# Joint gate-score levels and a four-quarter fp32 state readout in a hybrid RetNet/HGRN2 decoder step

## The chip, the cores and the metric

The kernel runs on one core of a Trainium2 chip. The metric is the device time of one execution in microseconds (us). TensorE (PE) does the matmuls; PEld are its weight loads; VectorE is DVE, ScalarE is ACT, GpSimd is POOL, and SyncE (SP) issues most of the transfers.

## The reference

One inference step of one decoder layer, in fp32, for 256 prompt tokens (one sequence) and 8 sample tokens (one new token of each of 8 running sequences). The model width is 2048.

```python
proj = rms_norm(x, norm_mix) @ w_in            # q,k,v,gate of retention; q,f,i,g of HGRN2; two merge gates
# retention, 8 heads, dk 128, dv 256, gamma_h = 1 - 2^(-5-h)
S = gamma * S + k^T v ;  o = q S               # per token; S starts at 0 (prompt) or at state_ret (samples)
# HGRN2, 8 heads, dk 128, dv 128
f = lb + (1 - lb) * sigmoid(z);  k = (1 - lb) * sigmoid(-z);  q = silu(hq)
S = diag(f) S + k^T i ;  o = S^T q
# both: RMS norm per head, swish gate, output projection; merged by two sigmoid gates, then w_out and residual
x = x + SwiGLU(rms_norm(x)) ;  y = rms_norm(x)
```

The new states (of the prompt and of each sample, for every head) are outputs too.

## The kernel before

The kernel keeps the activations transposed (features on 128 partitions, 264 tokens along the free axis: 256 prompt, then 8 sample tokens) and streams every weight matrix once, in chunks of 512 x 256 values (512 KB). SP loads a chunk into one of four ring slots (`raw`). ACT rounds it (`hi`, line 426), DVE forms the rest (`lo = raw - hi`, line 723), and PE multiplies hi*hi, hi*lo and lo*hi with 264 moving columns (lines 1082 to 1084): 24 matmuls for a chunk, in the reduced fp32r format, which streams a column per cycle. A slot is loaded again when DVE has split it, and `hi` is written again when PE has used the chunk.

The order of all work is written by hand. Each engine's program is a list of chunk numbers, with attention work hung behind certain chunks. The eight heads come first, 20 chunks ("steps" 0 to 19) each; head 0 stands apart and heads 1 to 7 are a loop. Then come the merge of both branches, the output projection and the feed-forward part. In a head:

- Step 3: DVE makes `forget`, `hkey`, `hquery` (lines 861 to 865) from PSUM, then hi/lo parts of the 8 sample keys and queries (`key_parts`, `query_parts`, lines 774 and 776), and spreads the query parts into a masked array with one used column per sample (`masked_query`, line 793). Step 7 does the same for retention. While step 3 runs, POOL norms the head before (lines 650 to 654) and then builds the gate products of this head.
- POOL (`levels`, lines 655 to 691): the causal decayed scores of HGRN2 are split into 7 levels. On level n, blocks of 2^n tokens look back at the block before. POOL forms `k_lev[n]` (keys of the first block of each pair times their decay; the other columns stay 0) and `q_lev[n]` for all 256 tokens, then the running products for the next level.
- SP loads the samples' old states `S_ret` (1 MB) and `S_hg` (512 KB) between the chunks of steps 13 and 14 (lines 371, 373).
- Steps 11 to 15 on PE: transposes of keys and values (line 1103), retention scores, the samples' rank-one updates (line 1113), outputs. Step 13's transposes wait for `v_parts` of DVE.
- Step 16 on PE: two diagonal score blocks (line 1187), then the level scores: 7 matmuls for the first 128 prompt tokens (line 1194) and 7 for the second 128 (line 1196). Each multiplies 128 columns of `k_lev` with all 128 columns of `q_lev`, of which 64 belong to its token block; DVE picks those with 7 predicated copies (line 934).
- Steps 14, 15, 17 on DVE: new sample states. ACT and DVE split them into `S_ret_hi/lo` and `S_hg_hi/lo` (lines 524, 532, 544, 809).
- Step 19 on PE, the readout (line 1224): for each of 8 samples and both parts of the state, one fp32r matmul of 16 stationary query columns (8 samples, hi and lo) with 256 (retention) or 128 (HGRN2) state columns, summed in PSUM rows 0 to 15. ACT copies these (`o16`, line 558). In the next head's step 0 (`tail`), PE turns them (lines 1124, 1126) and DVE adds the hi and lo rows (lines 817, 818).

```python
pe.wait_ge(state_split, h * 3 + 2)
for query, states, cols in ((q_only, (S_ret_hi, S_ret_lo), slice(0, RV)),
                            (hq_only, (S_hg_hi, S_hg_lo), slice(RV, 384))):
    for b in range(NS):
        for n, part in enumerate(states):
            last = mm(p7[0:2 * NS, 0, cols], query[:, b].rearrange("p c j -> p (c j)"), part[:, b, :], ...)
```

The large operands are placed at chosen address phases (`at_phase`), ahead of the heads' own arrays in memory.

Of the kernel before, what the change touches and what calls it, by code (L numbers as in the profile page):

```python
# [41 lines left out]
P = 128  # L42
# [45 lines left out]
K_IDENT = K_LEVEL + NLEV * 64  # L88
K_KDEC = K_IDENT + P
K_GAMMA = K_KDEC + 2 * H  # L90
K_EYE8 = K_GAMMA + H
K_ROW8 = K_EYE8 + NS * NS
# [14 lines left out]
def build(nc, consts, vectors, xT, w_in, w_ret, w_hg, w_out, w_fin, w_fout, s_ret, s_hg,  # L107
          yT, ret_p, hg_p, ret_s, hg_s):
    with ExitStack() as ctx:
# [35 lines left out]
        lb_tmp = alloc(heads, "lb_tmp", [P, 4, H])  # L145
        norm_tmp = ExitStack()
# [5 lines left out]
        hkey = alloc(heads, "hkey", [P, T])  # L152
        hquery = alloc(heads, "hquery", [P, T])
# [17 lines left out]
        q_parts = alloc(heads, "q_parts", [P, NS, 2], F32R)  # L171
        hq_parts = alloc(heads, "hq_parts", [P, NS, 2], F32R)

        q_only = alloc(heads, "q_only", [P, NS, 2, NS], F32R)
        hq_only = alloc(heads, "hq_only", [P, NS, 2, NS], F32R)
        o16 = alloc(heads, "o16", [2 * NS, 384])
# [8 lines left out]
        k_lev = [alloc(heads, f"k_lev{i}", [P, NP]) for i in range(NLEV)]  # L185
# [17 lines left out]
        S_ret_hi = alloc(heads, "S_ret_hi", [P, NS, RV], F32R)  # L203
        S_ret_lo = alloc(heads, "S_ret_lo", [P, NS, RV], F32R)
        S_hg_hi = alloc(heads, "S_hg_hi", [P, NS, HV], F32R)
        S_hg_lo = alloc(heads, "S_hg_lo", [P, NS, HV], F32R)
# [32 lines left out]
        c_level = cst[:, K_LEVEL:K_LEVEL + NLEV * 64].bitcast(I32).rearrange("p (l j) -> p l j", l=NLEV)  # L239
        c_kdec = cst[:, K_KDEC:K_KDEC + 2 * H].rearrange("p (b h) -> p b h", b=2)  # L240
        c_eye8 = cst[:, K_EYE8:K_EYE8 + NS * NS].rearrange("p (b j) -> p b j", b=NS)
# [41 lines left out]
        hg_sig_done = sem("hg_sig_done")  # L283
        products = sem("products")
# [6 lines left out]
        state_hi = sem("state_hi")  # L291
        state_split = sem("state_split")
# [120 lines left out]
        def _(act):  # L413
# [58 lines left out]
            def head(h, first=False):  # L472
# [3 lines left out]
                for i in range(HEAD_CHUNKS):  # L476
# [38 lines left out]
                    elif i == 15:  # L515

                        act.wait_ge(b_free, h * 2 + 3)
                        fn(hg_sig[:], hig[:, 1, :], ACT.Sigmoid).then_inc(hg_sig_done, 1)
# [4 lines left out]
                        act.wait_ge(p56_free, h * N56 + (OUT1 + 2))  # L523
                        copy(S_ret_hi[:, 0:4, :], S_ret[:, 0:4, :]).then_inc(state_hi, 1)
                    elif i == 16:
# [4 lines left out]

                        act.wait_ge(p56_free, h * N56 + (OUT1 + 3))
                        copy(S_ret_hi[:, 4:8, :], S_ret[:, 4:8, :]).then_inc(state_hi, 1)
                    elif i == 18:
# [8 lines left out]

                        act.wait_ge(p56_free, h * N56 + (OUTH4 + 2))
                        copy(S_hg_hi[:], S_hg[:]).then_inc(state_hi, 1)
                    elif i == 19:

                        act.wait_ge(a_free, h * 3 + 4)
                        fn(rg_sig[:], rg_gate[:], ACT.Sigmoid).then_inc(rg_sig_done, 1)


                        act.wait_ge(state_split, h * 3 + 3)
# [5 lines left out]
                        act.wait_ge(p7_full, h * N7 + (RD3 + 1))  # L557
                        copy(o16[:], p7[0:2 * NS, 0, 0:384]).then_inc(p7_free, 1)
# [65 lines left out]
        def _(pool):  # L624
            tt = nc.gpsimd.tensor_tensor
            pool.sem_inc(normed, 4)

# [15 lines left out]
            for i in range(NLEV):  # L643
                nc.gpsimd.memset(k_lev[i][:], 0.0).then_inc(products, 1)

            steps = 2 + 4 * NLEV + 4
# [10 lines left out]
            def levels(h):  # L657

                count = [NLEV]
# [13 lines left out]
                for i in range(NLEV):  # L673
# [6 lines left out]
                    shape = [P, NP // (2 * s), s]  # L680
# [3 lines left out]
                    step(tt(kl0, k0, g0, ALU.mult))  # L684
# [6 lines left out]
                step(tt(kbar, hkey[:, 0:NP], run_g[:], ALU.mult))  # L691
                assert count[0] == NLEV + steps
# [22 lines left out]
        def _(dve):  # L715
# [56 lines left out]
            def parts(hi_out, lo_out, x, h, n):  # L772

                nc.vector.tensor_copy(hi_out, x).then_inc(parts_done, 1)
                dve.wait_ge(parts_done, h * 14 + (2 * n + 1))
# [11 lines left out]
            def query_parts(out, x, h, n):  # L787
                parts(out[:, :, 0], out[:, :, 1], x, h, n)
# [14 lines left out]
            def level_psum(n):  # L803

                return bass.AP(tensor=p56, offset=64 * n, ap=[[2 * 512, P], [512 + 64, 2], [1, 64]])

            def state_lo(out, state, state_hi_part, h, n):
                dve.wait_ge(state_hi, h * 3 + (n + 1))
                tt(out, state, state_hi_part.bitcast(F32), ALU.subtract).then_inc(state_split, 1)

            def tail(i, h):

                if i == 0:

                    dve.wait_ge(p4_full, h * N4 + (TO4 + 1 - N4))
                    by_part = p4[:, 0, 0:48].rearrange("p (e two b) -> p e b two", e=3, two=2)
                    nc.vector.tensor_reduce(oT[:, :, NP:T], by_part[:, 0:2], AX.X, ALU.add).then_inc(sample_outputs, 1)
                    nc.vector.tensor_reduce(ohT[:, NP:T], by_part[:, 2], AX.X, ALU.add).then_inc(sample_outputs, 1)
# [8 lines left out]
            def head(h, first=False):  # L827
# [3 lines left out]
                for i in range(HEAD_CHUNKS):  # L831
# [26 lines left out]
                    if i == 3:  # L858
# [4 lines left out]
                        ts(hkey[:], z_nsig[:], omlb[:, bass.ds(h, 1)], None, ALU.mult).then_inc(forget_done, 1)  # L863
                        dve.wait_ge(a_free, h * 3 + 2)
# [3 lines left out]
                        query_parts(hq_parts, hquery[:, NP:T], h, 1)  # L868
                        dve.wait_ge(parts_done, h * 14 + 4)
                        masked_query(hq_only[:], hq_parts[:])  # L870
                    elif i == 7:
# [8 lines left out]
                        key_parts(k_parts, qk[:, 1, NP:T], h, 2)  # L880
                        query_parts(q_parts, qk[:, 0, NP:T], h, 3)
                        dve.wait_ge(parts_done, h * 14 + 8)
                        masked_query(q_only[:], q_parts[:])
                    elif i == 11:

                        dve.wait_ge(a_free, h * 3 + 3)
                        for e in range(2):
                            value_parts(v_parts[:, e], vT[:, e, NP:T], h, 4 + e)
                        dve.wait_ge(keys_copied, h + 1)
                        masked_keys(k_only[:], p7[0:8 * NS, 0, 256:384])  # L890
                        dve.wait_ge(masked, h * 3 + 3)
# [7 lines left out]
                    elif i in (14, 15):  # L899
# [9 lines left out]
                        if i == 15:  # L909

                            dve.wait_ge(b_free, h * 2 + 3)
                            value_parts(v_parts[:, 2], hig[:, 0, NP:T], h, 6)
                            state_lo(S_ret_lo[:, 0:4, :], S_ret[:, 0:4, :], S_ret_hi[:, 0:4, :], h, 0)
                    elif i == 16:
# [3 lines left out]
                           c_ident.rearrange("p (a n) -> p a n", a=1).broadcast_to([P, 2, P]), ALU.mult  # L918
                           ).then_inc(score_step, 1)
# [5 lines left out]
                        for n in range(NLEV):  # L925
# [4 lines left out]
                            msk = c_level[:, n:n + 1, :].rearrange("p a (b s) -> p a b s", s=s  # L930
                                                                   ).broadcast_to([P, 2, 64 // s, s])
# [4 lines left out]
                    elif i == 17:  # L936
# [7 lines left out]
                        state_lo(S_ret_lo[:, 4:8, :], S_ret[:, 4:8, :], S_ret_hi[:, 4:8, :], h, 1)  # L944
                    elif i == 18:
                        state_lo(S_hg_lo[:], S_hg[:], S_hg_hi[:], h, 2)

# [123 lines left out]
        def _(pe):  # L1071
# [26 lines left out]
            steps = 2 + 4 * NLEV + 4  # L1098

            def natural(out, src, width):  # L1100

                for b in range(2):
                    last = transpose(out[:, b * width:b * width + 128], src[:, b * P:b * P + P], c_ident)
# [5 lines left out]
            def sample_updates(q, h):  # L1109

                pe.wait_ge(masked, h * 3 + 3)
# [5 lines left out]
            def tail(i, h):  # L1117

                if i == 0:
# [3 lines left out]
                    one16 = c_ident[0:2 * NS, 0:2 * NS]  # L1123
# [12 lines left out]
            def attend(i, h):  # L1136

                if i == 11:

                    pe.wait_ge(p7_free, h * N7 + (TK0 + 1))  # L1140
                    pe.wait_ge(parts_done, h * 14 + 6)
# [7 lines left out]
                elif i == 13:  # L1149

                    pe.wait_ge(p56_free, h * N56 + (TV0 + 1))
                    pe.wait_ge(parts_done, h * 14 + 12)
# [24 lines left out]
                elif i == 16:  # L1177

                    pe.wait_ge(products, h * steps + (NLEV + steps))
                    pe.wait_ge(p7_free, h * N7 + (TI2 + 1))  # L1180
                    pe.wait_ge(parts_done, h * 14 + 14)
                    natural(p7[:, 0, 0:256], hig[:, 0, :], 128)
# [3 lines left out]
                    for b in range(2):  # L1186
                        mm(p4[:, 0, b * P:b * P + P], hkey[:, b * P:b * P + P], hquery[:, b * P:b * P + P],
                           start=True, stop=True)
# [194 lines left out]
```

## Time and profile before

| what | value |
|---|---|
| median of 3 runs (lowest to highest) | 1834.14 us (1831.59 to 1836.6) |
| the profiled execution's own time | 1834.16 us |
| its span, first to last instruction | 1832.3 us |
| mean granted TensorE clock | 0.995 |
| PE busy / PEld busy | 1785.3 us (97%) / 1766.0 us (96%) |
| DVE / ACT / POOL busy | 1147.5 (63%) / 776.9 (42%) / 277.4 us (15%) |
| HBM traffic over the span | 182 GB/s |

Matmuls are pipelined, and the duration of one record reaches past the start of the next. What a group of matmuls costs PE is therefore read from start to start. A matmul of plain fp32 operands shows as two records (each with its weight load), one of fp32r operands or a transpose as one. The name of an array in a row is without its number (`k_lev` for `k_lev0` to `k_lev6`; `p` for PSUM).

### The profile page before, as it was taken

How to read it: one execution, taken by the hardware profiler on the slowest of the kernel's cores; microseconds unless marked ns; L12 is line 12 of the kernel's file. 1: busy time of each engine (PE TensorE's matmuls, PEld its weight loads, DVE VectorE, ACT ScalarE, POOL GpSimd, SP SyncE). 2: the span in 40 equal slices, each digit the busy share in tenths (PEclk: the TensorE clock that was granted, in tenths of full speed). 3: DMA queues.
4: the chain of work that ended last, by engine and by line, in shares of the span. 5: the costliest groups of instructions: out<-in, count | busy, mean ns of one | idle time of the engine just before them, and what ended most of it. 6: DMA issues, size and time to landing. Idle time of an engine off the chain costs nothing.

```text
span 1832.3 us, 37809 instructions
## 1 busy us (share of the span) xinstructions
PE 1785.3 (97%) x14672; PEld 1766.0 (96%) x14672; DVE 1147.5 (63%) x1293; ACT 776.9 (42%) x894; POOL 277.4 (15%) x332
## 2 busy tenths in 40 slices
PE   5999999999999999999999999999999999999997
PEld 5999999999999999999999999999999999999996
DVE  8776877778777675555556665555555555545444
ACT  5454544445444454344444444444444444333332
POOL 4442614416144110000000000000000000000001
PEclk9999999999999999999999999999999999999998
DMA  7665646666466555555547665555565565555552
GB/s 230 192 202 177 197 139 197 190 183 196 140 193 191 184 163 185 184 183 183 182 153 245 192 183 183 182 180 181 181 182 182 183 182 182 185 184 177 179 182 102
DMA packets 388538, 333.86 MB, mean 182 GB/s; under 512 B 11776, under 2 KB 386560, under 8 KB 388352
## 3 DMA queue, kind: packets, MB, share of 16 engines
q1 hardware_dynamic: 369536, 318.88, 56.3%
q10 hardware_dynamic: 18944, 14.16, 2.5%
q8 instruction: 43, 0.70, 0.2%
q14 instruction: 15, 0.12, 0.0%
HBM read 316.67 MB, written 16.32 MB: 182 GB/s over the span
## 4 chain that ended last, share of the span: by engine, by line
PE 82%; DVE 7%; issue 4%; DMA 3%; SPq 2%; ACT 1%; DVEq 0%; POOL 0%; ACTq 0%
PE pA L1082 13%; PE pA L1084 12%; PE pA L1083 12%; PE pB L1082 10%; PE pB L1084 10%; PE pB L1083 10%; PE p L1082 3%; PE p L1084 3%; PE p L1083 3%; DMA raw<-in_w_in 2%; DVE lo L723 2%; PE p L1224 1%; SPq L348 1%; DVE hg_scores L934 1%; SPq L373 1%
## 5 line engine op out<-in xcount | busy, mean ns | idle before, releaser
L723 DVE TENSOR_TENSOR lo<-raw,hi 128x1024 fp32r<-128x1024 f32 x568 | 723.6, 1279 | 557.2 <-ACT hi L426 549.0
L426 ACT CAST hi<-raw 128x1024 fp32r<-128x1024 f32 x568 | 595.2, 1048 | 826.9 <-PE pA L1084 347.2
L1082 PE MATMUL pA<-h_hi,hi 128*128 128x264 f32 x1728 | 499.8, 289 | 19.0 <-DVE lo L723 18.7
L1083 PE MATMUL pA<-h_lo,hi 128*128 128x264 f32 x1728 | 492.0, 285 | 0.0
L1084 PE MATMUL pA<-h_hi,lo 128*128 128x264 f32 x1728 | 491.9, 285 | 0.0
L1082 PE MATMUL pB<-h_hi,hi 128*128 128x264 f32 x1472 | 421.6, 286 | 0.0
L1083 PE MATMUL pB<-h_lo,hi 128*128 128x264 f32 x1472 | 417.2, 283 | 0.0
L1084 PE MATMUL pB<-h_hi,lo 128*128 128x264 f32 x1472 | 417.2, 283 | 0.0
L1082 PEld LDWEIGHTS pA<-h_hi,hi 128*128 128x128 f32 x1728 | 327.7, 190 | 22.6 <-issue 18.9
L1083 PEld LDWEIGHTS pA<-h_lo,hi 128*128 128x128 f32 x1728 | 327.8, 190 | 0.3
L1084 PEld LDWEIGHTS pA<-h_hi,lo 128*128 128x128 f32 x1728 | 327.6, 190 | 0.0
L1082 PEld LDWEIGHTS pB<-h_hi,hi 128*128 128x128 f32 x1472 | 277.3, 188 | 0.3
L1083 PEld LDWEIGHTS pB<-h_lo,hi 128*128 128x128 f32 x1472 | 277.4, 188 | 0.2
L1084 PEld LDWEIGHTS pB<-h_hi,lo 128*128 128x128 f32 x1472 | 277.2, 188 | 0.0
L703 POOL TENSOR_TENSOR x<-x,vec 128x528 f32<-128x528 f32 x8 | 12.2, 1524 | 1151.2 <-DVE sq L1058 1151.2
L1082 PE MATMUL pA<-hid_hi,hi 128*128 128x264 f32 x352 | 99.9, 284 | 2.3 <-issue 2.3
L1082 PE MATMUL pB<-hid_hi,hi 128*128 128x264 f32 x352 | 100.3, 285 | 0.0
L1083 PE MATMUL pB<-hid_lo,hi 128*128 128x264 f32 x352 | 100.1, 284 | 0.0
L1084 PE MATMUL pB<-hid_hi,lo 128*128 128x264 f32 x352 | 100.1, 284 | 0.0
L1083 PE MATMUL pA<-hid_lo,hi 128*128 128x264 f32 x352 | 99.7, 283 | 0.0
L1084 PE MATMUL pA<-hid_hi,lo 128*128 128x264 f32 x352 | 99.5, 283 | 0.0
L1082 PE MATMUL p<-ro_hi,hi 128*128 128x264 f32 x256 | 72.7, 284 | 1.2 <-DVE ro_lo L979 1.2
(250 smaller groups left out, 2483.6 us busy)
## 6 DMA issues: line engine op xcount, KB each, us to landing
raw<-in_w_fin SPq DMA_DIRECT2D x176, 512.0 KB, 3.7
raw<-in_w_in SPq DMA_DIRECT2D x128, 512.0 KB, 3.5
raw<-in_w_in SPq DMA_DIRECT2D x192, 256.0 KB, 3.9
raw<-in_w_fout SPq DMA_DIRECT2D x88, 512.0 KB, 3.5
raw<-in_w_ret SPq DMA_DIRECT2D x32, 512.0 KB, 4.3
raw<-in_w_out SPq DMA_DIRECT2D x32, 512.0 KB, 4.2
S_ret<-in_s_ret SPq DMA_DIRECT2D x8, 1024.0 KB, 8.4
out_ret_s<-S_ret ACTq DMA_DIRECT2D x8, 1024.0 KB, 7.0
```

The lines of the kernel that those rows point to most:

```text
L348: sp.dma_start(raw[s][:, :, 0:128], half(i, first, col, 0)).then_inc(raw_full[s], 16)
L373: sp.dma_start(S_hg[:], s_hg[:, bass.ds(h, 1), :, :].rearrange("b h d e -> d (b h) e")).then_inc(state_in_hg, 16)
L426: copy(hi[s], raw[s]).then_inc(hi_done, 1)
L703: tt(x2[:, 2 * g:2 * g + 2, :], x2[:, 2 * g:2 * g + 2, :], vec[:, V_FINAL + 2 * g:V_FINAL + 2 * g + 2].rearrange("p (k a) -> p k a", a=1). ...
L723: tt(lo[s], raw[s], hi[s].bitcast(F32), ALU.subtract).then_inc(split_done, 1)
L934: last = nc.vector.copy_predicated(dst, msk, src)
L1082: mm(outs[t][:, ::-1], w_hi, a_hi[:, kt, ::-1], start=(kt == 0), stop=False)
L1083: mm(outs[t][:, ::-1], w_hi, a_lo[:, kt, ::-1], start=False, stop=False)
L1084: last = mm(outs[t][:, ::-1], w_lo, a_hi[:, kt, ::-1], start=False, stop=(kt == CK * n - 1))
L1224: last = mm(p7[0:2 * NS, 0, cols], query[:, b].rearrange("p c j -> p (c j)"), part[:, b, :], start=(b == 0 and n == 0), stop=(b == NS - 1 ...
```

## The change

Level scores. Both token blocks go into one matmul per level. The keys of the second 128 tokens are written in reverse order (`[:, ::-1]`), so that they fall on the columns that the first block's keys leave unused; `k_lev[n]` shrinks to 128 columns, nothing in it has to be zero, and its products are two half-size POOL instructions in place of one. The reversed keys and values of the second block come from two new arrays: `hkey_back` (DVE, step 3) and `hval_back` (ACT, step 15, which PE's step 16 waits for). The masks, no longer the same for both blocks, get twice as wide in the constants, and the second diagonal block uses a reversed identity.

Readout. The states stay in plain fp32, so their four splits and the two query splits go. The 8 samples are put into four groups of 32 stationary columns. Group g writes PSUM rows 32g to 32g+31 through `tile_position=(0, 32 * g)`, first for sample g, then, summed, for sample 4+g. The query arrays are cleared once at the start and DVE then writes only the 8 used columns of each. ACT copies 128 rows, PE turns them with three full transposes, and DVE copies the used columns instead of adding pairs. ACT issues the two state stores after that copy and no longer before it.

```diff
-            def masked_query(out, q):
-                shape = [P, NS, 2, NS]
-                tt(out, q.bitcast(F32).rearrange("p b (c a) -> p b c a", a=1).broadcast_to(shape),
-                   c_eye8.rearrange("p b (a j) -> p b a j", a=1).broadcast_to(shape), ALU.mult).then_inc(masked, 1)
+            def place_queries(out, q):
+                return nc.vector.tensor_copy(
+                    out[:, :, 0:128].rearrange("p r (g j) -> p r g j", g=4)[:, :, :, 0],
+                    q.rearrange("p (r g) -> p r g", r=2)).then_inc(queries_placed, 1)
...
                         ts(hkey[:], z_nsig[:], omlb[:, bass.ds(h, 1)], None, ALU.mult).then_inc(forget_done, 1)
+                        ts(hkey_back[:], z_nsig[:, P:NP][:, ::-1], omlb[:, bass.ds(h, 1)], None, ALU.mult)
                         dve.wait_ge(a_free, h * 3 + 2)
                         tt(hquery[:], hqf[:, 0, :], hq_sig[:], ALU.mult).then_inc(forget_done, 1)
                         dve.wait_ge(forget_done, h * 3 + 3)
                         key_parts(hk_parts, hkey[:, NP:T], h, 0)
-                        query_parts(hq_parts, hquery[:, NP:T], h, 1)
-                        dve.wait_ge(parts_done, h * 14 + 4)
-                        masked_query(hq_only[:], hq_parts[:])
+                        place_queries(hq_only, hquery[:, NP:T])
...
-                    step(tt(kl0, k0, g0, ALU.mult))
+                    tt(kl0, k0[:, 0:n], g0[:, 0:n], ALU.mult).then_inc(products, 1)
+                    step(tt(kl1, k0[:, n:], g0[:, n:], ALU.mult))
...
                     for n in range(NLEV):
-                        mm(p56[:, 0, 64 * n:64 * n + P], k_lev[n][:, 0:P], q_lev[n][:], start=True, stop=True)
-                    for n in reversed(range(NLEV)):
-                        last = mm(p56[:, 1, 64 * n:64 * n + P], k_lev[n][:, P:NP], q_lev[n][:], start=True, stop=True)
+                        last = mm(p56[:, n // 4, (n % 4) * P:(n % 4) * P + P], k_lev[n][:], q_lev[n][:],
+                                  start=True, stop=True)
...
-                        copy(S_hg_hi[:], S_hg[:]).then_inc(state_hi, 1)
-                        state_lo(S_hg_lo[:], S_hg[:], S_hg_hi[:], h, 2)
...
-                    pe.wait_ge(state_split, h * 3 + 2)
+                    pe.wait_ge(queries_placed, h * 2 + 2)
+                    pe.wait_ge(p56_free, h * N56 + (OUTH4 + 2))
+                    for query, state, cols in ((q_only, S_ret, slice(0, RV)), (hq_only, S_hg, slice(RV, 384))):
+                        rows = query[:].rearrange("p r x -> p (r x)")
+                        for r in range(2):
+                            for g in range(4):
+                                b = 4 * r + g
+                                last = mm(p7[32 * g:32 * g + 32, 0, cols], rows[:, 32 * b:32 * b + 32], state[:, b, :],
+                                          start=(r == 0), stop=(r == 1), tile_position=(0, 32 * g))
...
-                    mm(p4[:, 0, 0:16], o16[:, 0:128], one16, start=True, stop=True)
-                    for e in range(1, 3):
-                        last = transpose(p4[:, 0, 16 * e:16 * e + 16], o16[:, e * 128:e * 128 + 128], one16)
+                    for e in range(3):
+                        last = transpose(p4[:, 0, e * P:e * P + P], o_rows[:, e * P:e * P + P], c_ident)
```

## Rows read from the trace of the kernel before

Heads are numbered 0 to 7. The stretches of rows 3 run from ACT's first square root in one head's step 2 to the same place in the next.

**Rows 1.** the page's part 1: busy time of each engine

```profile
PE 1785.3 (97%) x14672; PEld 1766.0 (96%) x14672; DVE 1147.5 (63%) x1293; ACT 776.9 (42%) x894; POOL 277.4 (15%) x332
```

**Rows 2.** the list of waits, engine PE: line, releaser, us in total, times, longest

```profile
PE p L1103 <- DVE v_parts L776: 8.2, 6, 1.6
...
PE p L1203 <- DVE hg_scores L934: 1.9, 8, 0.3
```

**Rows 3.** stretches of head 1 and head 7: us, busy by engine

```profile
107.40:182.50 75.10, 74.72 (x610) 72.69 (x609) 56.22 (x78) 35.57 (x49) 31.29 (x38) 1.00 0.63 185
...
565.60:642.40 76.80, 74.96 (x610) 72.71 (x609) 56.85 (x78) 35.53 (x49) 29.79 (x38) 1.00 0.59 180
```

**Rows 4.** chain that ended last, head 7 from step 14: start us, us, what

```profile
609.35 0.43 PE p L1170 x2
...
615.62 1.56 PE p L1194 x14
...
630.09 2.84 PE p L1224 x32
```

**Rows 5.** timeline of PE at step 14: start us, us, instruction

```profile
604.45 0.28 PE L1084 MATMUL pB<-h_hi,lo 128*128 128x264 f32 x1
604.66 0.74 PE L1113 MATMUL p<-v_rows,k_only 32*128 32x256 f32 x4
605.33 1.13 PE L1164 MATMUL p<-v_nat,kd_nat 128*128 128x256 f32 x4
```

**Rows 6.** timeline of PE, step 19: readouts of 256, then 128 columns

```profile
553.11 0.28 PE L1224 MATMUL p<-S_ret_hi,q_only 128*16 128x256 f32 x1
...
554.99 0.22 PE L1224 MATMUL p<-S_hg_hi,hq_only 128*16 128x128 f32 x1
```

**Rows 7.** weight loads of the readout: ns min/median/max, first and last start

```profile
L1224 PEld LDWEIGHTS p<-S_ret_hi,q_only x64: 93/95/96, 94.8 to 631.5; 128*16 128x16 f32 x64
```

**Rows 8.** timeline of PE: transposes of step 11, then of the tail

```profile
592.36 0.28 PE L1084 MATMUL pA<-h_hi,lo 128*128 128x264 f32 x1
...
592.48 0.38 PE L1103 MATMUL p<-cst,qk 128*128 128x128 f32 x2
...
592.93 0.28 PE L1083 MATMUL pB<-h_lo,hi 128*128 128x264 f32 x1
...
635.59 0.28 PE L1084 MATMUL pA<-h_hi,lo 128*128 128x264 f32 x1
...
636.47 0.28 PE L1083 MATMUL pA<-h_lo,hi 128*128 128x264 f32 x1
```

**Rows 9.** chain that ended last, head 7, between steps 3 and 14

```profile
589.27 6.07 DMA raw<-in_w_in
```

**Rows 10.** timeline of DVE in step 3, head 1, then head 7

```profile
117.49 0.42 DVE L865 TENSOR_TENSOR hquery<-hqf,hq_sig 128x264 f32<-128x264 f32 x1
...
120.70 5.49 DVE L723 TENSOR_TENSOR lo<-raw,hi 128x1024 fp32r<-128x1024 f32 x4
...
575.37 0.35 DVE L863 TENSOR_SCALAR hkey<-z_nsig,omlb 128x264 f32<-128x264 f32 x1
...
575.64 1.55 DVE L865 TENSOR_TENSOR hquery<-hqf,hq_sig 128x264 f32<-128x264 f32 x1
...
578.24 0.67 DVE L774 CAST hq_parts<-hquery 128x8 fp32r<-128x8 f32 x1
...
579.57 5.48 DVE L723 TENSOR_TENSOR lo<-raw,hi 128x1024 fp32r<-128x1024 f32 x4
```

**Rows 11.** groups by line and shape: DVE's split of the new states

```profile
L809 DVE TENSOR_TENSOR S_ret_lo<-S_ret,S_ret_hi 128x1024 fp32r<-128x1024 f32 x16 | 19.5, 1221 | 0.0
```

**Rows 12.** timelines, head 7: POOL, last product; PE, step 16

```profile
602.58 1.60 POOL L691 TENSOR_TENSOR rg_sig<-hkey,run_g 128x256 f32<-128x256 f32 x1
...
614.24 0.38 PE L1103 MATMUL p<-cst,hig 128*128 128x128 f32 x2
```

**Rows 13.** DMA issues: queue, count, KB each, median us to landing

```profile
cst<-in_consts SPq DMA_DIRECT2D x1, 1888.0 KB, 9.0
```

More of the change, by code:

```diff
@@ L145, in build @@
         lb_tmp = alloc(heads, "lb_tmp", [P, 4, H])
+        q_only = alloc(heads, "q_only", [P, 2, NS * 16 + 1])
+        hq_only = alloc(heads, "hq_only", [P, 2, NS * 16 + 1])
         norm_tmp = ExitStack()
@@ L152, in build @@
         hkey = alloc(heads, "hkey", [P, T])
+        hkey_back = alloc(heads, "hkey_back", [P, P])
+        hval_back = alloc(heads, "hval_back", [P, P])
         hquery = alloc(heads, "hquery", [P, T])
@@ L184, in build @@
         S_hg = alloc(heads, "S_hg", [P, NS, HV])
-        k_lev = [alloc(heads, f"k_lev{i}", [P, NP]) for i in range(NLEV)]
+        k_lev = [alloc(heads, f"k_lev{i}", [P, P]) for i in range(NLEV)]
         run_f = alloc(heads, "run_f", [P, NP])
@@ L517, in head @@
                         act.wait_ge(b_free, h * 2 + 3)
+                        copy(hval_back[:], hig[:, 0, P:NP][:, ::-1]).then_inc(hval_turned, 1)
                         fn(hg_sig[:], hig[:, 1, :], ACT.Sigmoid).then_inc(hg_sig_done, 1)
@@ L642, in _ @@
             pool.wait_ge(h_done, 4)
-            for i in range(NLEV):
-                nc.gpsimd.memset(k_lev[i][:], 0.0).then_inc(products, 1)
-            steps = 2 + 4 * NLEV + 4
+            steps = 2 + 5 * NLEV + 5
             def last_outputs(h):
@@ L679, in levels @@
                     kl0, _ = halves(k_lev[i][:], s)
-                    shape = [P, NP // (2 * s), s]
+                    kl1, _ = halves(k_lev[i][:, ::-1], s)
+                    n, shape = P // (2 * s), [P, NP // (2 * s), s]
                     if i:
@@ L690, in levels @@
                 step(tt(run_g[:, 0:P], run_g[:, 0:P], run_f[:, NP - 1:NP].broadcast_to([P, P]), ALU.mult))
-                step(tt(kbar, hkey[:, 0:NP], run_g[:], ALU.mult))
-                assert count[0] == NLEV + steps
+                tt(kbar[:, 0:P], hkey[:, 0:P], run_g[:, 0:P], ALU.mult).then_inc(products, 1)
+                count[0] += 1
+                step(tt(kbar[:, P:NP][:, ::-1], hkey[:, P:NP], run_g[:, P:NP], ALU.mult))
+                assert count[0] == steps
             levels(0)
@@ L803, in level_psum @@
             def level_psum(n):
[L805 to L809, printed above, removed]
+                return p56[:, n // 4, (n % 4) * P:(n % 4) * P + P].rearrange("p (k j) -> p k j", k=2)
             def tail(i, h):
@@ L1096, in _, with natural @@
                 pe.sem_inc(free, 1)
-            steps = 2 + 4 * NLEV + 4
-            def natural(out, src, width):
+            steps = 2 + 5 * NLEV + 5
+            def natural(out, src, width, second=None):
                 for b in range(2):
-                    last = transpose(out[:, b * width:b * width + 128], src[:, b * P:b * P + P], c_ident)
+                    block = src[:, b * P:b * P + P] if second is None or b == 0 else second
+                    last = transpose(out[:, b * width:b * width + 128], block, c_ident)
                 return last
@@ L1177, in attend @@
                 elif i == 16:
-                    pe.wait_ge(products, h * steps + (NLEV + steps))
+                    pe.wait_ge(products, h * steps + steps)
                     pe.wait_ge(p7_free, h * N7 + (TI2 + 1))
-                    pe.wait_ge(parts_done, h * 14 + 14)
-                    natural(p7[:, 0, 0:256], hig[:, 0, :], 128)
+                    pe.wait_ge(parts_done, h * 10 + 10)
+                    pe.wait_ge(hval_turned, h + 1)
+                    natural(p7[:, 0, 0:256], hig[:, 0, :], 128, second=hval_back[:])
                     natural(p7[:, 0, 256:512], kbar, 128).then_inc(p7_full, 1)
@@ L1186, in attend @@
                     for b in range(2):
-                        mm(p4[:, 0, b * P:b * P + P], hkey[:, b * P:b * P + P], hquery[:, b * P:b * P + P],
-                           start=True, stop=True)
+                        mm(p4[:, 0, b * P:b * P + P], hkey_back[:] if b else hkey[:, 0:P],
+                           hquery[:, b * P:b * P + P], start=True, stop=True)
                     mm(p4[:, 0, 256:384], k_top, q_lev[NLEV][:], start=True, stop=True)
@@ L1215, in attend @@
                 elif i == 19:
-                    pe.wait_ge(state_split, h * 3 + 2)
-                    for query, states, cols in ((q_only, (S_ret_hi, S_ret_lo), slice(0, RV)),
-                                                (hq_only, (S_hg_hi, S_hg_lo), slice(RV, 384))):
-                        if query is hq_only:
-                            pe.wait_ge(state_split, h * 3 + 3)
-                        for b in range(NS):
-                            for n, part in enumerate(states):
-                                last = mm(p7[0:2 * NS, 0, cols], query[:, b].rearrange("p c j -> p (c j)"),
-                                          part[:, b, :], start=(b == 0 and n == 0), stop=(b == NS - 1 and n == 1))
+                    pe.wait_ge(queries_placed, h * 2 + 2)
[7 more added lines that the diff above has]
+                                          start=(r == 0), stop=(r == 1), tile_position=(0, 32 * g))
                     last.then_inc(p7_full, 1)
```

90 lines of the change are left out of this document (37 added, 53 removed).

## The prediction

> **What bounds the kernel now.** I read the page first. PE is busy for 1785.3 of 1832.3 us [rows 1], so what counts is which matmuls go, and where PE still waits. The list of PE's waits has, past the start, one large entry: step 13's transposes wait 8.2 us for DVE's `v_parts`, and 1.9 us are waited for the predicated copies [rows 2]. The windows by head place the first: head 1 takes 75.1 us, head 7 76.8 with the same PE work, and heads 2 to 6 are like head 7 (76.4 to 76.8) [rows 3]. Everything else that the change takes from DVE and ACT lies beside a busy PE. All edits lie in the eight heads, the first 640 us or so; after them nothing changes.
>
> **Level scores.** PE runs 14 records (7 fp32 matmuls) at line 1194 in 1.56 us, and as many at line 1196 [rows 4]. One set goes; the other keeps its shape, 128 by 128. 8 x 1.56 = **-12.5 us**. PE is next busy with chunk 17, so nothing takes the gap. DVE's copies start at the end of the last level matmul as before, and the 1.9 us behind them stay. POOL gets eight more instructions in a head (seven levels and `kbar`, each product in two halves). Its last product ends at 604.2 and PE first needs them at 614.24 [rows 12]: 10 us of cover, enough even at 1.2 us for each addition; beyond that PE would wait at step 16 one for one. `hval_back` is a small ACT copy early in step 15, covered by chunk 16 (24 matmuls at 0.12 us = 2.9 us) and by the ACT cast of the state that leaves the same step. Both at nothing. The wider masks make the constants 256 KB larger; at 1888 KB in 9.0 us [rows 13] that is 1.2 us in front of chunk 4's load, three chunks ahead of PE's need of it: between 0 and +1.2, I take 0.
>
> **Readout.** Before: 32 fp32r matmuls in 2.84 us [rows 4], 0.1175 us apart where they stream 256 columns ((554.99 - 553.11) / 16 [rows 6]). After: 16 plain fp32 matmuls, that is 32 records. Plain fp32 costs 0.43 / 2 = 0.215 us per record at 256 columns (line 1170) and 1.56 / 14 = 0.111 at 128 [rows 4]. One behind the other: 16 x 0.215 + 16 x 0.111 = 5.22 us. All four quarters side by side: a quarter, 1.31 us. No row shows two column groups at work at once, so these are the two ends. Between them: records start in program order in every timeline, and the two records of one matmul use the same 32 columns. The second then waits out the first, and the next group's first record, queued behind it, can only run beside that second one. So matmuls pair up: 8 x 0.215 + 8 x 0.111, and a last record of 0.111, = 2.72 us. A change to a narrower tile also costs: line 1113's four matmuls, 0.47 us at the pace above, take 0.76 (from 604.45 + 0.12 to 605.33 [rows 5]). That is 0.29 more, so 1.60, 3.01 or 5.51 us. I take the pairing, 3.01, since the two-record form and the order of starts are what the rows show: 8 x (3.01 - 2.84) = **+1.4 us**, with ends at -9.9 and +21.4.
>
> The Trainium skill ("TensorE: Matmul & The Clock Gate", section "Part 3: Packing small matmuls — row/col tiling") says that matmuls on different column groups run concurrently while starting in strict program order, and gives 2.38 times for three column tiles. By that factor the readout would be 5.22 / 2.38 + 0.29 = 2.48 us and the whole kernel an estimated 1811.3; no run here shows it, and the order of starts is the part that the timelines agree with. It is rival 1 below with a smaller factor and shares its chance.
>
> **Turning the outputs.** Three transposes of 128 x 128 in step 11 stretch two steps of PE (0.24 us) to 592.93 - 592.36 = 0.57: 0.33 us. The small ones of the tail stretch them to 636.47 - 635.59 = 0.88: 0.64 us [rows 8]. The change puts the former in place of the latter: 8 x -0.31 = **-2.5 us**. DVE's copies replace reductions of the same few columns: nothing.
>
> **The splits.** DVE loses three passes of 1.22 us in a head [rows 11], ACT three casts. They stand in steps 15 to 18, where PE waits for the predicated copies only: nothing. Step 19's wait moves from the splits to the new HGRN2 state of step 17 and the placed queries of steps 3 and 7, all done a chunk earlier; behind it PE holds the next head's chunk 0, and no wait at line 1224 stood there before. ACT's two stores now come behind the readout. The next load of these states is over 40 us later, and ACT's next cast waits for chunk 0 anyway: nothing.
>
> **The wait at step 13.** The chain runs from DVE's step 3 to the `lo` that frees the slot (579.57 [rows 10]), to SP, which queues the states' 1.5 MB ahead of chunk 14, to that chunk's landing 6.07 us after 589.27 [rows 9], and to `v_parts`. Whatever shortens step 3 shortens it. In head 1 `hquery` took 0.42 us, in head 7 1.55, because POOL's last products ran against it; from its start to the next `lo` it was 3.21 against 3.93 us, 0.72 apart [rows 10], and the head was 1.7 us shorter [rows 3]. So 1 us of step 3 is worth some 2.4. The change removes the query parts and their mask, 579.57 - 578.24 = 1.33 us. It adds the placing, at most the 0.67 of the cast of the same 128 x 8, and `hkey_back`, 128 of the 264 columns of `hkey` (0.35 us), 0.17 [rows 10]. Net -0.49, times 2.4, times six heads = -7.0. `hkey_back` stands just where `hquery` was held, though, and may be held itself. If it adds the full 1.13 of that hold, step 3 grows by 0.64 and seven heads lose 10.6 us. The best end is the whole 8.2 gone. More likely one hold takes the place of the other; I take **-5 us**. What is late next is the same chunk's transfer.
>
> **Sum.** -12.5 + 1.4 - 2.5 - 5 = -18.6. The profiled execution took 1834.16 us (span 1832.3), within 0.1 us of the median 1834.14: **1815.6 us**.
>
> **The rivals.**
> 1. All four quarters run side by side. For: the groups have different columns, states and PSUM rows. Against: the two records of each matmul and the order of starts. Readout 1.60 us, -9.9: 1804.3 us.
> 2. The change doesn't do what it says: fp32 records with a tile position run one behind the other. For: each needs its own stream of state columns, and no row shows two streams. Readout 5.51 us, +21.4, which eats the level scores and the rest: 1835.6 us, no change.
> 3. Slower: as 2, and no weight load is hidden, since the columns' owner changes with every matmul. In the trace these loads (95 ns at 16 columns [rows 7]) lie beside the matmul before. Exposed, 32 x 0.095 = 3.0 us more, 8.55 in all: 8 x 5.71 = +45.7, so 1859.9 us. It decides from a readout of 6.0 us on (8 x 3.2 = 25.5 eats the 20 us saved elsewhere and 5.5 more). Against: line 1113's narrow tile keeps the pace within the 0.29 us above.
> 4. The wait at step 13 grows: `hkey_back` is held by POOL for as long as `hquery` was. +10.6 in place of -5: 1831.2 us. Against: `hquery` then starts after POOL's long products and is held less.
>
> **How the numbers follow.** Pairing 0.45, side by side 0.25, serial 0.18, serial with exposed loads 0.07, the grown wait 0.05. A measurement of this kernel can tell about 0.3% (5.5 us) from no change. Faster by more: nearly all of the first two, with little of the third, 0.72. Within: most of the serial case, part of the grown wait and of pairing, 0.16. Slower: the exposed loads and the rest of the serial case, 0.12. The likeliest alone spans 1808 to 1824 (the step-13 term from -8 to 0, the rest from the readout). The range, 1802 to 1839, takes in rivals 1, 2 and 4 and leaves out rival 3.
>
> **What would show it.** Line 1194's group at 14 records in a head in some 1.56 us, and no second group. The readout from its first record to chunk 0's next: near 3.0 us (pairing), 1.6 (four at once), 5.5 or more (serial); the starts of the records tell which: in pairs, all at once, or 0.215 apart. The tail's transposes at 0.33 us. Line 1103's wait on `v_parts` at some 3 us in place of 8.2, with step 3 shorter by about half a us. No new wait of PE at step 16 on POOL or `hval_back`. It is wrong if the readout is over 5 us, or if heads 2 to 7 don't get shorter than 75 us.

## The result, and the profile after

The changed kernel takes 1806.66 us (median of 4 executions, 1805.17 to 1807.51) against 1834.34 us for the kernel before (median of 4, 1831.59 to 1836.6): a ratio of 0.9849 [0.9832, 0.9866], 27.7 us less. That is inside the range on record and 8.9 us below the predicted 1815.6; rival 1's figure, 1804.3, is the nearest one. It lies outside the 1808 to 1824 that the prediction gave its likeliest case: the range holds it because it took in rival 1.

The profiled execution took 1805.17 us with a span of 1803.4 us, 28.9 us less than the span before. First its busy times (page, part 1), beside [rows 1]:

```profile
PE 1757.9 (97%) x14552; PEld 1738.9 (96%) x14552; DVE 1102.5 (61%) x1245; ACT 751.8 (42%) x878; POOL 296.2 (16%) x391
```

PE's busy time fell by 27.4 us, nearly the whole gain; PE's waits changed too, longer in one place and shorter in another. The list of PE's waits (line, releaser, us in total, times, longest), beside [rows 2]:

```profile
PE p L1180 <- DVE hg_scores L915: 4.2, 8, 0.7
PE p L1082 <- DVE v_parts L766: 3.9, 5, 1.5
```

The wait of step 13 went from 8.2 to 3.9 us; the one behind DVE's predicated copies from 1.9 to 4.2. The stretches of heads 1 and 7 (window, its length, busy us of PE, PEld, DVE, ACT and POOL, clock, DMA share, GB/s), beside [rows 3]:

```profile
105.20:177.90 72.70, 71.66 (x596) 69.49 (x595) 51.58 (x72) 32.50 (x47) 32.41 (x46) 1.00 0.64 191
...
541.20:614.20 73.00, 71.67 (x596) 69.49 (x595) 51.35 (x72) 32.50 (x46) 32.67 (x46) 1.00 0.62 190
```

Head 7 lost 3.8 us and head 1 lost 2.4, so the two are now nearly alike. Heads 2 to 6 are no longer than head 7, so all came below the 75 us that the prediction set as a sign. The heads end at 614.2 us where they ended at 642.4, and what follows them takes 1189.2 us where it took 1189.9: the gain lies in the heads, as predicted.

**The readout.** PE's part of the chain that ended last in the changed kernel (start us, us, what), beside the last row of [rows 4]; the second row is the chunk's next matmul, and the last is the turning of the outputs in the next head's first step:

```profile
602.41 1.44 PE p L1201 x32
603.85 0.32 PE pA L1060
...
606.97 0.33 PE p L1103 x3
```

PE's timeline of the same readout (start us, us, instruction), with, below the second "...", rows of two narrow windows, which show a few of the 32 records each; beside [rows 6]:

```profile
602.13 0.28 PE L1062 MATMUL pA<-h_hi,lo 128*128 128x264 f32 x1
602.35 1.07 PE L1201 MATMUL p<-S_ret,q_only 128*32 128x256 f32 x16
603.23 0.62 PE L1201 MATMUL p<-S_hg,hq_only 128*32 128x128 f32 x16
603.78 0.39 PE L1060 MATMUL pA<-h_hi,hi 128*128 128x264 f32 x1
604.01 0.28 PE L1061 MATMUL pA<-h_lo,hi 128*128 128x264 f32 x1
...
602.35 0.42 PE L1201 MATMUL p<-S_ret,q_only 128*32 128x256 f32 x4
...
603.02 0.40 PE L1201 MATMUL p<-S_ret,q_only 128*32 128x256 f32 x4
```

Records start four at once. The batches of 256 columns start at 602.35, 602.59, 602.80 and 603.02, that is some 0.22 us apart, the pace that one record alone has at line 1170 [rows 4]. The 16 HGRN2 records follow in four batches 0.11 us apart. With the pace of its neighbours taken off (0.12 us from 602.13, and again before 604.01), the readout takes (604.01 - 0.12) - (602.13 + 0.12) = 1.64 us. The chain gives the same: 1.44, and 0.20 by which the row after it is longer than the 0.12 of its neighbours. In the kernel before, the row after the readout was only 0.05 longer, so there it took 2.84 + 0.05 = 2.89 us:

```profile
632.93 0.17 PE pA L1082
```

### The profile page after: what moved, and what is told of

It is laid out like the page before. It is cut to its first block, busy times and chain, and to the rows that moved or that the text cites. A ratio compares the mean times of both kernels' runs of the same rounds, so it can differ in the third digit from the quotient of the medians.

```text
span 1803.4 us, 37531 instructions
## 1 busy us (share of the span) xinstructions
PE 1757.9 (97%) x14552; PEld 1738.9 (96%) x14552; DVE 1102.5 (61%) x1245; ACT 751.8 (42%) x878; POOL 296.2 (16%) x391
## 4 chain that ended last, share of the span: by engine, by line
PE 83%; DVE 6%; issue 4%; DMA 2%; SPq 2%; ACT 2%; DVEq 0%; POOL 0%; ACTq 0%
PE pA L1060 13%; PE pA L1062 13%; PE pA L1061 13%; PE pB L1060 11%; PE pB L1062 11%; PE pB L1061 11%; PE p L1060 3%; PE p L1062 3%; PE p L1061 3%; DMA raw<-in_w_in 2%; DVE lo L713 1%; SPq L342 1%; ACT hi L420 1%; DVE hg_scores L915 1%; PE p L1201 1%
```

## The experiments

The edits are to the changed kernel, except in the first two, where a part of the change is made alone in the kernel before, and in the last, which builds on experiment 8. Of each edit only the lines that matter are shown. The kernel before ran again beside them, with medians from 1834.9 to 1836.0 us, and each ratio is against those runs; a wait is that of the one execution that was profiled.

**1. The level scores alone.** The joint levels with the reversed keys, values and masks, cut to the lines on PE:

```diff
 for n in range(NLEV):
-    mm(p56[:, 0, 64 * n:64 * n + P], k_lev[n][:, 0:P], q_lev[n][:], start=True, stop=True)
-for n in reversed(range(NLEV)):
-    last = mm(p56[:, 1, 64 * n:64 * n + P], k_lev[n][:, P:NP], q_lev[n][:], start=True, stop=True)
+    last = mm(p56[:, n // 4, (n % 4) * P:(n % 4) * P + P], k_lev[n][:], q_lev[n][:],
+              start=True, stop=True)
```

> The kernel before with the joint level scores alone (old readout, old splits). If the level scores return a part of their 12.5 us at the wait for the predicated copies (1.9 us before, 4.2 after) and hkey_back lengthens step 3 of DVE, with no query work removed there: -12.5 + 2.3 + 3 to 6, so 1827 to 1830 us. Rival: the level scores are worth their full 12.5 us by themselves, and the longer wait came with the readout: 1822 us, line 1203's counterpart waiting about 1.9 us.

Measured: 1824.92 us against 1835.7, ratio 0.9937 [0.9924, 0.9951], so 10.8 us less. PE's waits:

```profile
PE p L1111 <- DVE v_parts L784: 9.5, 7, 2.6
PE p L1211 <- DVE hg_scores L941: 4.0, 8, 0.7
```

The time lies between the two expectations, so it doesn't decide; the second row does. Taking out one set of 14 records makes the wait behind the copies 4.0 us (1.9 before): 12.5 - 2.1 = 10.4 us of gain. Of the 3 to 6 us that step 3 was expected to cost, the first row shows 1.3 (9.5 us, 8.2 before), no more than runs of one kernel differ by (experiment 5).

**2. The readout alone.** Plain states, placed queries, four quarters and the large transposes, without the joint levels:

```diff
-                        for b in range(NS):
-                            for n, part in enumerate(states):
-                                last = mm(p7[0:2 * NS, 0, cols], query[:, b].rearrange("p c j -> p (c j)"),
-                                          part[:, b, :], start=(b == 0 and n == 0), stop=(b == NS - 1 and n == 1))
+                        rows = query[:].rearrange("p r x -> p (r x)")
+                        for r in range(2):
+                            for g in range(4):
+                                b = 4 * r + g
+                                last = mm(p7[32 * g:32 * g + 32, 0, cols], rows[:, 32 * b:32 * b + 32], state[:, b, :],
+                                          start=(r == 0), stop=(r == 1), tile_position=(0, 32 * g))
```

> The kernel before with the four-quarter fp32 readout alone (old level scores). If the four quarters run side by side: readout some 1.5 us a head in place of 2.84 (-9.9), turning -2.5, the wait at step 13 gone for want of hkey_back (up to -8.2): about 1814 us. Rival: the readout itself is no faster, and the gain came from the level scores and the splits: -2.5 and a part of -8.2, 1826 us or more.

Measured: 1819.03 us, ratio 0.9912 [0.9897, 0.9927]. PE's waits, then the readout in the chain:

```profile
PE p L1074 <- DVE v_parts L758: 5.5, 6, 1.1
PE p L1172 <- DVE hg_scores L908: 2.0, 8, 0.3
```

```profile
615.14 1.44 PE p L1193 x32
```

The readout is the same 1.44 us, and the wait behind the copies stays at 2.0, so its growth belongs to the levels alone. The time is 5 us above the 1814 that I expected: I let the wait of step 13 go entirely, and 5.5 us of it stayed, as much as the miss. The product of the two ratios, 0.9937 x 0.9912 = 0.9850, is the ratio of the whole change (0.9849) within its interval: the parts add and don't help each other.

**3. No quarters.** The same plain fp32 matmuls with 128 stationary columns, of which one is used, and no tile position:

```diff
-                                last = mm(p7[32 * g:32 * g + 32, 0, cols], rows[:, 32 * b:32 * b + 32], state[:, b, :],
-                                          start=(r == 0), stop=(r == 1), tile_position=(0, 32 * g))
+                                last = mm(p7[:, 0, cols], rows[:, P * b:P * b + P], state[:, b, :],
+                                          start=(b == 0), stop=(b == 7))
```

> The changed kernel with the same 16 fp32 matmuls on the full array: stationary operands of 128 columns (one used column for each sample), no tile position, one after another. If the quarters side by side are what made the readout short, it takes 16 x 0.215 + 16 x 0.111 = 5.2 us a head in place of 1.5 and the kernel takes 1835 us. Rival: the quarters don't overlap and fp32 records are cheap in this place for another reason: within 5 us of 1807.

Measured: 1834.52 us, ratio 0.9994 [0.9985, 1.0004]: the change without its quarters is worth nothing. The chain's row:

```profile
625.43 5.24 PE p L1201 x32
```

That is the prediction's serial figure (5.22); the time is also the one that rival 2 gave, though this edit drops the tile position, which rival 2 kept. The row after it is as short as its neighbours, so the readout is 5.24 us, and the quarters save 5.24 - 1.64 = 3.60 us in a head, 28.8 in eight; the times differ by 27.9.

**4. The order of the quarters.** This one aims at the step that failed. If records start in program order, and the two records of a matmul can't run at once, then with all four records of a group one behind the other the groups can hardly overlap:

```diff
-                        for r in range(2):
-                            for g in range(4):
+                        for g in range(4):
+                            for r in range(2):
```

> The changed kernel with the two loops of the readout swapped: both samples of a quarter directly behind each other. If a matmul that waits for its own quarter holds up all behind it (program order of starts), a quarter's second matmul starts 0.43 us after its first and the next quarter only beside it: 5 x 0.43 + 5 x 0.22 = 3.2 us in place of 1.5, +14 us, 1820 us. If each quarter takes its matmuls from the queue by itself, nothing changes: 1807 us.

Measured: 1806.81 us, ratio 0.9840 [0.9825, 0.9855], the time of the changed kernel. The readout in the chain, then a narrow window of PE's timeline at its start:

```profile
606.40 1.48 PE p L1201 x32
```

```profile
606.34 0.44 PE L1201 MATMUL p<-S_ret,q_only 128*32 128x256 f32 x4
```

Four records start at once again, though the first four in the program all belong to group 0 and write the same 32 PSUM rows. The whole still takes 1.48 us, where starts in program order, with a group's records one behind the other, were to take 3.2. So the program's order doesn't set the order of starts across column groups, and the assumption behind the pairing is wrong. The rows don't name a record's group, so one rival is left: that four records of one group run together. The spread of the starts speaks against it. A record alone lasts 0.40 us, so the first four starts lie within 0.04 us here (0.44) and within 0.02 in the changed kernel (0.42). That is twice as far, as it would be for the first matmuls of the four groups, which here stand two places apart in the program and there next to each other.

**5. The changed kernel again**, as the base for the next three, on their chip; no edit.

> The changed kernel itself once more, beside the next three: 1807 us, waits at step 13 between 2 and 6 us in total and at step 17 some 4.2 us.

Measured: 1807.06 us (1804.89 to 1809.28), ratio 0.9843 [0.9829, 0.9856]; its waits were 5.1 us (step 13) and again 4.2 us (behind the copies), its span 1805.4:

```profile
PE p L1082 <- DVE v_parts L766: 5.1, 6, 2.1
```

The wait at step 13 thus differs between executions: 3.9 and 5.1 in one kernel, and 6.4 in experiment 4, where nothing near step 3 differs. Only differences well above that can be read.

**6. A split behind the copies.** In step 16 DVE makes the `lo` of chunk 20 before it turns to the scores; here it does so after the predicated copies:

```diff
-                    split_lo(4 + i, c + (4 + i), 1)
+                    if i != 16:
+                        split_lo(4 + i, c + (4 + i), 1)
...
+                        split_lo(20, c + 20, 1)
```

> The changed kernel with DVE's split of chunk 20 moved in step 16 from ahead of the score work to behind the predicated copies. If that split is what makes PE wait longer at step 17 since the level scores got shorter, the wait falls from 4.2 us to about 2 (copies of 0.29 + 2.83 us against 2.9 us of chunk 17) and the kernel takes 1804.5 us. Rival: the later split holds up the loads behind it, and PE waits for a chunk instead: 1807 us or more, with a wait at line 1060 on DVE's lo inside the heads.

Measured: 1804.42 us (1802.93 to 1804.65), ratio 0.9825 [0.9812, 0.9839]; all its executions lie below all of experiment 5. PE's waits:

```profile
PE p L1084 <- DVE v_parts L766: 2.8, 4, 0.8
PE p L1182 <- DVE hg_scores L916: 1.8, 8, 0.3
```

To see why, DVE's timeline of step 16 in the changed kernel:

```profile
589.13 1.23 DVE L713 TENSOR_TENSOR lo<-raw,hi 128x1024 fp32r<-128x1024 f32 x1 [2.35 <-ACT hi L420]
590.27 0.41 DVE L900 TENSOR_TENSOR hg_scores<-p,cst 128x256 f32<-128x256 f32 x1
...
591.11 0.29 DVE L906 COPY hg_scores<-p 128x128 f32<-128x128 f32 x1
591.32 2.83 DVE L915 COPY_PREDICATED hg_scores<-cst,p 128x128 f32<-128x128 int32 x7
```

and in this experiment:

```profile
589.14 0.29 DVE L907 COPY hg_scores<-p 128x128 f32<-128x128 f32 x1 [0.82 <-PE p L1174]
589.35 2.83 DVE L916 COPY_PREDICATED hg_scores<-cst,p 128x128 f32<-128x128 int32 x7
592.09 2.35 DVE L713 TENSOR_TENSOR lo<-raw,hi 128x1024 fp32r<-128x1024 f32 x2
```

In the changed kernel no row between the split and the copies has a release in brackets but the split itself, which waited 2.35 us for ACT's cast: DVE ran late behind ACT, not behind PE. In the kernel before, the row ahead of the copies did wait for PE's last level scores (line 1196), for 1.39 us:

```profile
618.78 0.29 DVE L924 COPY hg_scores<-p 128x128 f32<-128x128 f32 x1 [1.39 <-PE p L1196]
```

With the split moved, that row waits for PE's scores again (0.82 us, released by L1174), and PE's wait is back at 1.8 us.

**7. The reversed key later.** `hkey_back` moves from step 3, where the chain to step 13 begins, to step 9:

```diff
-                        ts(hkey_back[:], z_nsig[:, P:NP][:, ::-1], omlb[:, bass.ds(h, 1)], None, ALU.mult)
...
+                    elif i == 9:
+                        ts(hkey_back[:], z_nsig[:, P:NP][:, ::-1], omlb[:, bass.ds(h, 1)], None, ALU.mult)
```

> The changed kernel with hkey_back moved on DVE from step 3 to step 9. If hkey_back's own 1.3 us lengthen step 3 and so the wait at step 13, step 3 gets up to 1 us shorter, that wait goes and the kernel takes some 1803 us. Rival: POOL's products hold whichever DVE instruction stands there, hquery takes 1.55 us again as before the change, step 3 is 0.2 us shorter at most and the time stays within 1.5 us of 1807.

Measured: 1803.59 us (1802.12 to 1807.53), ratio 0.9828 [0.9815, 0.9842]. The wait of step 13, and DVE's `hkey`, `hquery` and the next split in step 3:

```profile
PE p L1083 <- DVE v_parts L766: 1.8, 4, 0.6
```

```profile
549.36 0.35 DVE L848 TENSOR_SCALAR hkey<-z_nsig,omlb 128x264 f32<-128x264 f32 x1
549.63 1.55 DVE L850 TENSOR_TENSOR hquery<-hqf,hq_sig 128x264 f32<-128x264 f32 x1
...
552.56 3.80 DVE L713 TENSOR_TENSOR lo<-raw,hi 128x1024 fp32r<-128x1024 f32 x3
```

The wait lost 3.3 us and the time 3.5, but the executions overlap with those of experiment 5, so the size is uncertain. DVE's step 3 shows that the hold returned to `hquery` (1.55 us): from `hkey` at 549.36 to this split it is 3.20 us, where the changed kernel takes 3.42, so only 0.22 us went, not the whole of the instruction moved. Step 3 came out as the rival had it and the time as the first expectation had it; the prediction's factor of 2.4 would make 3.2 us of 0.22 us in six heads, but executions that overlap can't show it.

**8. Both.** Experiments 6 and 7 together.

> Both moves of the two runs before in one kernel. If they act at different places, their gains add: 1801 to 1805 us. Rival: what is saved at one wait is lost at the other, since the states' load and chunk 14 come when they come: 1806 to 1807 us.

Measured: 1801.35 us (1800.63 to 1802.59), ratio 0.9815 [0.9801, 0.9828], 5.7 us below experiment 5 with no overlap, and near the sum of the two gains (2.6 and 3.5). PE's waits:

```profile
PE p L1183 <- DVE hg_scores L917: 1.8, 8, 0.3
PE p L1085 <- DVE v_parts L766: 1.8, 2, 1.2
```

This version beats both kernels: the change, with the two DVE instructions moved.

**9. Two halves.** Column groups of 64 in place of 32, so two at once:

```diff
-                        for r in range(2):
-                            for g in range(4):
+                        for r in range(4):
+                            for g in range(2):
...
-                                          start=(r == 0), stop=(r == 1), tile_position=(0, 32 * g))
+                                          start=(r == 0), stop=(r == 3), tile_position=(0, 64 * g))
```

> The changed kernel with two groups of 64 stationary columns in place of four of 32 (tile positions 0 and 64, four samples summed in each). If groups run side by side without regard to the order of the queue, the readout takes half of the serial 5.24 us, 2.6, and with the change of tile some 2.8 in place of 1.6: +9 us, 1816 us. Rival: only the 32-column tile runs groups at once, and two halves go one after the other: 5.5 us, 1837 us.

Measured: 1815.94 us against 1834.94, ratio 0.9894 [0.9878, 0.9909]. The chain's rows:

```profile
615.24 2.75 PE p L1201 x32
617.99 0.32 PE pA L1060
```

With the row after it, 0.20 us longer than its neighbours as in the changed kernel, the readout is 2.95 us. Four groups took 1.64 us, that is the prediction's serial sum of 5.22 us divided by 4, and 0.34 for the narrow tiles. With the same 0.34, two groups should take 5.22 / 2 + 0.34 = 2.95 us: as measured.

**10. POOL waits.** Experiment 8, and POOL starts its last products of the head before (`ret_o`, `hg_o`) only when DVE has made this head's `hquery`:

```diff
             def last_outputs(h, last=False):
...
+                if not last:
+                    pool.wait_ge(forget_done, h * 3 + 3)
```

> The kernel with both late moves, and POOL's last two products of the head before (ret_o, hg_o) made to wait until DVE has hquery. If those products are what holds DVE's step 3, hquery takes 0.42 us and not 1.55, the place of step 3 gets about 1 us shorter, and the wait at step 13 (1.8 us left) goes: 1799 to 1800 us. Rival: something else holds DVE there (hquery stays at 1.5), or POOL's products then hold the next DVE passes as long: 1801 us or more.

Measured: 1801.59 us, ratio 0.9817 [0.9803, 0.9831], the time of experiment 8. DVE's groups of instructions by shape (us busy, mean ns | idle before), here:

```profile
L768 DVE TENSOR_TENSOR key_pair<-hkey,key_pair 128x16 fp32r<-128x16 f32 x8 | 9.6, 1206 | 0.3
...
L853 DVE TENSOR_TENSOR hquery<-hqf,hq_sig 128x264 f32<-128x264 f32 x8 | 3.4, 419 | 0.0
```

and in experiment 8:

```profile
L851 DVE TENSOR_TENSOR hquery<-hqf,hq_sig 128x264 f32<-128x264 f32 x8 | 11.3, 1411 | 0.0
...
L766 DVE TENSOR_TENSOR key_pair<-hkey,key_pair 128x16 fp32r<-128x16 f32 x8 | 3.6, 453 | 0.3
```

`hquery` is 992 ns shorter when POOL's products come later, and `key_pair`'s subtraction is then held instead (753 ns more), with the splits behind it (5.88 us for four; 5.27 in experiment 8). That POOL's products hold DVE is shown; that moving them gives time is refuted here. There was little left to win too: the wait of step 13, 1.8 us in experiment 8, is 1.6.

## Why the prediction was right or wrong

| term | predicted | measured | from |
|---|---|---|---|
| level scores | -12.5 | -12.5 + 2.3 | 14 records gone in each head; wait at L1180 |
| readout | +1.4 | -10.0 | 8 x (1.64 - 2.89) |
| turning | -2.5 | -2.4 | 8 x (0.34 - 0.64) |
| wait of step 13 | -5 | -4.3 | 8.2 to 3.9 |
| after the heads | 0 | -0.7 | 1189.9 to 1189.2 |

The measured terms sum to -27.6 us of the span's -28.9. The other 1.3 us I can't assign; two profiled executions of the changed kernel differ by 2.0.

**Readout: wrong, and the mechanism with it.** The step that failed is "the next group's first record, queued behind it, can only run beside that second one". The four quarters run side by side from the first record on, as rival 1 had it: 1.64 us (1.60 worked out there, 3.01 by the pairing I chose). Experiment 3 shows that without quarters the matmuls run one behind the other. Experiment 9 shows that two groups halve the time. Experiment 4 shows that the order of samples in the program plays no part. The order of starts was one of the two reasons that I gave against rival 1. It came from timelines in which all matmuls use all the columns or, one after another, the same ones (the first 16 at line 1224). These show that such records keep their order and say nothing on groups that don't touch each other. The other reason, the two records of each matmul, holds at most within a group: the batches are 0.22 us apart, and the other groups don't wait. The terms of rival 1 were right: the record paces, and nearly the 0.29 us for narrow tiles (0.34 measured), though that one was read at line 1113, whose matmuls are narrow in rows and use all columns. That the sum came within 9 us all the same is no merit of the pairing, which put the readout at +1.4 us where it gave -10.0.

The Trainium skill ("TensorE: Matmul & The Clock Gate", section "Part 3: Packing small matmuls — row/col tiling") says that matmuls start and end strictly in program order. Experiment 4 speaks against that for these matmuls of two records each, on different column groups: 1.48 us in the other order. Its factor of 2.38 for three column tiles has no counterpart here; four gave 5.24 / 1.64 = 3.2 with the tile change in it.

**Level scores: right at PE, wrong behind it.** 14 records remain and take 1.5 us. PE's timeline in step 16:

```profile
589.07 1.73 PE L1172 MATMUL p<-q_lev,k_lev 128*128 128x128 f32 x14
590.55 0.37 PE L1060 MATMUL pA<-h_hi,hi 128*128 128x264 f32 x1
```

The failed step is "the 1.9 us behind them stay". DVE did not simply follow PE: with one set of records gone, PE was done with the scores at 590.55. DVE had only just ended the split of chunk 20 (590.36), which starts with ACT's cast and not with the scores, and the rest of its own score work still stood ahead of the copies. Experiment 1 shows the cost and experiment 6 its cause (2.1 and 2.4 us over eight heads). The prediction had asked what DVE waits for after the matmuls, not what DVE does just ahead of them.

**Step 13: the direction right, the size by its own hedge.** DVE's step 3 in the changed kernel, head 7, beside [rows 10]:

```profile
550.01 0.34 DVE L848 TENSOR_SCALAR hkey<-z_nsig,omlb 128x264 f32<-128x264 f32 x1
550.28 1.34 DVE L849 TENSOR_SCALAR hkey_back<-z_nsig,omlb 128x128 f32<-128x128 f32 x1
551.54 1.00 DVE L851 TENSOR_TENSOR hquery<-hqf,hq_sig 128x264 f32<-128x264 f32 x1
...
553.11 0.67 DVE L779 COPY hq_only<-hquery 128x8 f32<-128x8 f32 x1
553.43 5.27 DVE L713 TENSOR_TENSOR lo<-raw,hi 128x1024 fp32r<-128x1024 f32 x4
```

and POOL's timeline beside it:

```profile
550.14 1.40 POOL L638 TENSOR_TENSOR ret_o<-oT,rg_gate 128x528 f32 x1 [0.20 <-POOL ohT L636]
551.50 0.76 POOL L639 TENSOR_TENSOR hg_o<-ohT,hg_gate 128x264 f32 x1
```

From `hkey` to the split it is 3.42 us, 0.78 less than the 4.20 of before, where 0.49 was expected: `hkey_back` is held (1.34 us, ending with `ret_o`), and `hquery`, 1.00 us, less than the 1.55 it had. So "one hold takes the place of the other" holds, and rival 4's growth didn't come. The wait fell by 4.3 us, while executions with the same step 3 differ by 2.5 here: the factor of 2.4 is neither confirmed nor refuted. Experiment 10 shows that POOL is the cause of the hold.

The Trainium skill ("SBUF — State Buffer", section "🔬 SBUF: two separate sides") has VectorE and GpSimd share a port pair, an exclusive lock that one instruction keeps to its end; on VectorE's side it concerns instructions in a 2-port mode or with two SBUF inputs. Experiment 10's `hquery`, 419 ns in place of 1411, agrees: both its inputs, `hqf` and `hq_sig`, are SBUF arrays, not PSUM as the description of step 3 has it. `hkey_back` has one input array; which mode it ran in no run here shows.

**Right as they stood:** the turning; and the items priced at nothing: PE's list of waits has no new one at step 16 on POOL or `hval_back`, none at the readout, and none on the longer constants (the wait at the start, 21.0 us before, is 21.9, but 22.3 in experiment 2, whose constants are the short ones).

## What to carry to other kernels

A set of small plain fp32 matmuls that leave TensorE's columns idle can be worth placing on column groups: four groups turned a change worth nothing (1834.5 us) into one worth 28 us, in either of two orders. When a group of matmuls goes, look at what the consuming engine does just ahead of it: what was hidden behind the matmuls becomes the wait, and moving it gave 2.6 us here. A rule about order that was read from instructions that share a resource should not be carried to instructions that don't.

## What was not expected of the hardware

Plain fp32 matmuls of two records each run at once on four column groups, and the time goes with 1/n: 5.24, 2.95 and 1.64 us for one, two and four groups, 0.34 us of it for the narrow tiles in the last two. The records start four at a time in both orders of the program that were tried. And a hold of DVE by POOL is not removed when one instruction is moved away from it; it passes to the next DVE instructions (`hquery` from 1411 to 419 ns, `key_pair` from 453 to 1206).
